# Second attention of a two-block layer: probabilities and values in rounded part and remainder, three rounded products for one fp32 product

## What is computed

```
def attend(args):
    qb, qc = args
    s = jnp.einsum('bqhd,bkhd->bhqk', qb, k).astype(jnp.float32) * scale
    mask = cid[None, :] <= qc[:, None]
    s = jnp.where(mask[None, None], s, neg)
    p = jax.nn.softmax(s, axis=-1).astype(v.dtype)
    return jnp.einsum('bhqk,bkhd->bqhd', p, v)
...
return o * jax.nn.silu(z)
...
y = jnp.concatenate([y_conv, y_mla, y_ret], axis=-1)
h = h + y @ w_out[l]
```

## Time and profile before

| | us |
|---|---|
| median of three runs (1928.8 to 1929.09) | 1928.89 |
| the profiled execution | 1929.18 |
| its span, first to last instruction | 1927.4 |
| PE busy in the span | 1859.5 |
| DVE busy | 1189.0 |
| ACT busy | 784.2 |
| POOL busy | 552.8 |

### The profile page before, as it was taken

One profiled execution on the slowest core, in us unless ns is written; L12 is line 12 of the kernel. 1 busy time (PEld: TensorE's weight loads), 2 busy tenths in 40 slices (PEclk: granted clock), 3 DMA queues, 4 the chain that ended last, 5 costly groups with the idle time before them and its releaser, 6 DMA issues.

```text
span 1927.4 us, 24207 instructions
## 1 busy us (share of the span) xinstructions
PE 1859.5 (96%) x9462; PEld 1512.4 (78%) x9462; DVE 1189.0 (62%) x1805; ACT 784.2 (41%) x1404; POOL 552.8 (29%) x554
## 2 busy tenths in 40 slices
PE   8999999899988999999999998999999998899999
PEld 5788788766777888887888887879988897676787
DVE  6678545555788666777877877455344348466642
ACT  6765223455543333333333354451211136455520
POOL 0120026440637565610000024560622134011100
PEclk9999999999999999999999999999999999899999
DMA  4143433300314535479555401113101314311131
GB/s 160 47 148 102 148 88 105 110 31 26 133 60 156 177 129 172 142 285 397 197 182 212 174 1 32 44 59 136 40 23 44 110 60 142 110 34 34 44 131 66
DMA packets 110026, 216.27 MB, mean 112 GB/s; under 512 B 37512, under 2 KB 42888, under 8 KB 105816
## 3 DMA queue, kind: packets, MB, share of 16 engines
q1 hardware_dynamic: 109624, 214.49, 32.8%
q10 hardware_dynamic: 288, 0.22, 0.0%
HBM read 153.82 MB, written 60.87 MB: 111 GB/s over the span
## 4 chain that ended last, share of the span: by engine, by line
PE 74%; DVE 10%; ACT 6%; POOL 4%; issue 3%; DMA 2%; SPq 0%; DVEq 0%; POOLq 0%; ACTq 0%
PE ps L361 10%; PE ps L362 9%; PE ps L363 9%; PE ps L1948 5%; PE ps L1950 5%; PE ps L1949 5%; PE ps L2336 5%; PE ps L2338 5%; PE ps L2337 5%; PE ps L3653 4%; PE ps L378 3%; PE ps L706 2%; ACT sc L1502 1%; PE ps L3554 1%; PE ps L3642 1%
## 5 line engine op out<-in xcount | busy, mean ns | idle before, releaser
L361 PE MATMUL ps<-xh,whi 128*128 128x512 f32 (+2 forms) x1160 | 458.3, 395 | 10.1 <-DVE wlo L330 6.4
L362 PE MATMUL ps<-xl,whi 128*128 128x512 f32 (+2 forms) x1160 | 442.9, 382 | 0.0
L363 PE MATMUL ps<-xh,wlo 128*128 128x512 f32 (+2 forms) x1160 | 442.1, 381 | 0.0
L361 PEld LDWEIGHTS ps<-xh,whi 128*128 128x128 f32 x1160 | 220.3, 190 | 59.6 <-issue 11.8
L363 PEld LDWEIGHTS ps<-xh,wlo 128*128 128x128 f32 x1160 | 219.9, 190 | 39.9
L362 PEld LDWEIGHTS ps<-xl,whi 128*128 128x128 f32 x1160 | 220.3, 190 | 33.1
L1948 PE MATMUL ps<-oph,wsh 128*128 128x512 f32 x448 | 177.2, 396 | 11.2 <-DVE stu L2066 6.0
L2336 PE MATMUL ps<-dnh_b,dnh_a 128*128 128x512 f32 x448 | 175.2, 391 | 5.0 <-DVE dn_b L2362 5.0
L1949 PE MATMUL ps<-opl,wsh 128*128 128x512 f32 x448 | 176.4, 394 | 0.0
L1950 PE MATMUL ps<-oph,wsl 128*128 128x512 f32 x448 | 176.2, 393 | 0.0
L2337 PE MATMUL ps<-dn_b,dnh_a 128*128 128x512 f32 x448 | 174.8, 390 | 0.0
(11 more groups left out here) (515 smaller groups left out, 3402.9 us busy)
## 6 DMA issues: line engine op xcount, KB each, us to landing
wraw<-panels SPq DMA_DIRECT2D x70, 512.0 KB, 3.6
dnr_b<-ff_d SPq DMA_DIRECT2D x28, 1024.0 KB, 7.5
dnr_a<-down SPq DMA_DIRECT2D x28, 1024.0 KB, 5.1
ff_d<-st SPq DMA_DIRECT2D x64, 256.0 KB, 5.9
ff_d<-stt SPq DMA_DIRECT2D x48, 256.0 KB, 5.9
upx<-up SPq DMA_DIRECT2D x16, 512.0 KB, 3.8
upy<-up SPq DMA_DIRECT2D x16, 512.0 KB, 5.5
hT<-x SPq DMA_DIRECT2D x8, 512.0 KB, 5.0
```

The lines of the kernel that those rows point to most:

```text
L361: pe.matmul(out, h, xh[:, xk, c0:c1_], start=(n == 0), stop=False)
L362: pe.matmul(out, h, xl[:, xk, c0:c1_], start=False, stop=False)
L363: mm = pe.matmul(out, l, xh[:, xk, c0:c1_], start=False, stop=(n == nk - 1))
```

## The change

Each unit is exponentiated twice by ACT: into a rounded buffer ("exp high", six buffers ph) and into an fp32 buffer (three pt). POOL subtracts one from the other and writes the remainder, rounded (three buffers pl, "p low"). The values of two heads are split once: ACT writes the rounded part vh, POOL the remainder vl, before head 0 and in slots 5 and 6 of heads 0, 2 and 4. PE makes high x high and high x low of unit j - 2 and the product of the low probabilities of unit j - 4 in each slot. The copies of sums move from ACT to DVE (slots 4 and 9), the inverses of half 1 to slots 5 to 8 and, in the last head, ahead of y_low of k = 0, 1 and 5; the ten early pieces of y move by four slots; POOL's multiplies are put between its subtractions; SP issues all eight hr loads after the last attention product. The lines of the changed kernel are 40 to 90 higher than before.

```diff
@@ -3501,7 +3501,14 @@
...
-    pts = [X(f"pt{i}", 37888 + 2048 * i, [512]) for i in range(4)]
+    pts = [X(f"pt{i}", 37888 + 2048 * i, [512]) for i in range(3)]
+    phs = [X("ph0", 44032, [512], F32R)] + [X(f"ph{i + 1}", 20096 + 2048 * i, [512], F32R) for i in range(5)]
+    pls = [X("pl0", 30336, [512], F32R)] + [X(f"pl{i + 1}", 59904 + 2048 * i, [512], F32R) for i in range(2)]
+    phs7 = [phs[0]] + [M(f"ph7{i}", 28 + 2 * i, [512], F32R) for i in range(5)]
+    pls7 = [M(f"pl7{i}", 38 + 2 * i, [512], F32R) for i in range(3)]
...
+    vhs = [X("vh0", 46080, [NB + 1, 3, 64], F32R), M("vh1", 80.1875, [NB + 1, 3, 64], F32R)]
+    vls = [X("vl0", 52992, [NB + 1, 3, 64], F32R), at("vl1", c_at, [NB + 1, 3, 64], F32R)]
...
+    def p_high(j):
+        return (phs7 if j // nu == 7 else phs)[j % 6]
+
+    def p_low(j):
+        return (pls7 if j // nu == 7 else pls)[j % 3]
...
+    def value_high_act(act, w, c):
...
+        step = 1 if c < 2 else 2
+        for n, bs in value_parts:
+            act.activation(vhs[c % 2][0:n, bs, 0:3:step, :], vm[0:n, bs, c, 0:3:step, :], ACT.Copy).then_inc(*act_at.up("vh", c, n))
+
+    def value_low_pool(pool, w, c):
...
+        step = 1 if c < 2 else 2
+        for n, bs in value_parts:
+            w.wait_ge(*act_at.at("vh", c, n))
+            pool.tensor_tensor(vls[c % 2][0:n, bs, 0:3:step, :], vm[0:n, bs, c, 0:3:step, :], vhs[c % 2][0:n, bs, 0:3:step, :].bitcast(F32), ALU.subtract).then_inc(*pool_at.up("vl", c, n))
...
-        def values(j):
+        def values_high(j):
             h, u = j // nu, j % nu
             hf, x, c0 = units[u]
+            c, n = h // 2, n_keys(x)
             if x == 0:
-                take(w, "values", ("o", h, hf), (act_at, ("o", h, hf)))
-            w.wait_ge(*act_at.at("exp", h, u))
-            w.wait_ge(*pool_la.at("ones"))
-            pe.matmul(tile("o", h, hf)[:, c0:512], values_of(h, x), pts[j % 4][0:n_keys(x), 0:512 - c0], start=(x == 0), stop=(x == last_x[hf])
-                      ).then_inc(*pe_at.up("values", j))
+                take(w, "values", ("o", h, hf), (dve_at, ("o", h, hf)))
+            w.wait_ge(*act_at.at("exp high", h, u))
+            w.wait_ge(*pool_at.at("vl", c, NMETA))
+            o = tile("o", h, hf)
+            pe.matmul(o[:, c0:512], vhs[c % 2][0:n, x, h % 2:h % 2 + 2, :], p_high(j)[0:n, 0:512 - c0], start=(x == 0), stop=False, skip_group_check=True)
+            pe.matmul(o[:, c0:512], vls[c % 2][0:n, x, h % 2:h % 2 + 2, :], p_high(j)[0:n, 0:512 - c0], start=False, stop=False, skip_group_check=True)
+
+        def values_low(j):
+            h, u = j // nu, j % nu
+            hf, x, c0 = units[u]
+            c, n = h // 2, n_keys(x)
+            w.wait_ge(*pool_at.at("p low", j))
+            pe.matmul(tile("o", h, hf)[:, c0:512], vhs[c % 2][0:n, x, h % 2:h % 2 + 2, :], p_low(j)[0:n, 0:512 - c0], start=False, stop=(x == last_x[hf]),
+                      skip_group_check=True).then_inc(*pe_at.up("values", j))
+                j = nu * h + u
                 scores(h, u)
-                if nu * h + u >= 2:
-                    values(nu * h + u - 2)
+                if j >= 2:
+                    values_high(j - 2)
+                if j >= 4:
+                    values_low(j - 4)
                 if h < 7:
                     for step in prepare[u]:
                         prepare_pe(pe, w, h + 1, *step)
-                elif u < 4:
-                    y_turn_pe(pe, w, *early[u])
-        values(8 * nu - 2)
-        values(8 * nu - 1)
+                elif 4 <= u < 8:
+                    y_turn_pe(pe, w, *early[u - 4])
+        values_high(8 * nu - 1)
+        for j in range(8 * nu - 3, 8 * nu):
+            values_low(j)
...
     def attend_act(act, w):
+        value_high_act(act, w, 0)
+        for h in range(8):
+            for u in range(nu):
+                hf, x, c0 = units[u]
+                j, n = nu * h + u, n_keys(x)
+                p = tile("unit", h, u)[0:n, 0:512 - c0]
+                w.wait_ge(*pe_at.at("unit", h, u))
+                if j > 5:
+                    w.wait_ge(*pe_at.at("values", j - 6))
+                act.activation(p_high(j)[0:n, 0:512 - c0], p, ACT.Exp).then_inc(*act_at.up("exp high", h, u))
+                if j > 2:
+                    w.wait_ge(*pool_at.at("p low", j - 3))
+                act.activation(pts[j % 3][0:n, 0:512 - c0], p, ACT.Exp).then_inc(*act_at.up("exp", h, u))
+                if h % 2 == 0 and h < 6 and u == 5:
+                    value_high_act(act, w, h // 2 + 1)
+                if h < 7:
+                    for step in prepare[u]:
+                        prepare_act(act, w, h + 1, *step)
+                elif 4 <= u < 4 + len(early):
+                    w.wait_ge(*pe_at.at("values", 7 * nu - 1))
+                    y_high_act(act, w, *early[u - 4])
+        for k in (0, 1, 5):
+            y_high_act(act, w, k, 0)
+
+    def attend_dve(dve, w):
                 w.wait_ge(*pool_at.at("y", h // 2 - 1, hf))
-            act.activation(den[hf][a:a + 64, :], p[b:b + 64, :], ACT.Copy).then_inc(*act_at.up("den", h, hf))
-            act.activation(og[hf][a:a + 64, :], p[a:a + 64, :], ACT.Copy).then_inc(*act_at.up("o", h, hf))
...
-                j = nu * h + u
...
-                act.activation(pts[j % 4][0:n_keys(x), 0:512 - c0], tile("unit", h, u)[0:n_keys(x), 0:512 - c0], ACT.Exp).then_inc(*act_at.up("exp", h, u))
-                if u == 2 and h > 0:
-                    summed(h - 1, 1)
-                if u == 7:
-                    summed(h, 0)
-                if h < 7:
-                    for step in prepare[u]:
-                        prepare_act(act, w, h + 1, *step)
-                elif u < len(early):
-                    y_high_act(act, w, *early[u])
-        for k in (0, 1, 5):
-            y_high_act(act, w, k, 0)
-        summed(7, 1)
-
-    def attend_dve(dve, w):
+            dve.tensor_copy(den[hf][a:a + 64, :], p[b:b + 64, :]).then_inc(*dve_at.up("den", h, hf))
+            dve.tensor_copy(og[hf][a:a + 64, :], p[a:a + 64, :]).then_inc(*dve_at.up("o", h, hf))
+
...
@@ -3708,29 +3767,61 @@
                 if h < 7:
                     for step in prepare[u]:
                         prepare_dve(dve, w, h + 1, *step)
-                if h > 0 and h % 2 == 0 and 3 <= u < 7:
-                    inverse(h // 2 - 1, 1, u - 3)
+                if u == 4 and h > 0:
+                    summed(h - 1, 1)
+                if u == 9:
+                    summed(h, 0)
+                if h > 0 and h % 2 == 0 and 5 <= u < 9:
+                    inverse(h // 2 - 1, 1, u - 5)
                 if h > 0 and h % 2 == 1 and u >= 10:
                     inverse(h // 2, 0, u - 10)
-                if h == 7 and u < len(early):
-                    y_low_dve(dve, w, *early[u])
+                if h == 7 and 4 <= u < 4 + len(early):
+                    y_low_dve(dve, w, *early[u - 4])
+        summed(7, 1)
+        for n in range(4):
+            inverse(3, 1, n)
         for k in (0, 1, 5):
             if k > 0:
                 w.wait_ge(*pe_at.end())
             y_low_dve(dve, w, k, 0)
-        for n in range(4):
-            inverse(3, 1, n)
 
     def attend_pool(pool, w):
-        for c in range(4):
...
+        def gated(c, hf):
...
+        value_low_pool(pool, w, 0)
+        for h in range(8):
+            for u in range(nu):
+                hf, x, c0 = units[u]
+                j, n = nu * h + u, n_keys(x)
+                w.wait_ge(*act_at.at("exp", h, u))
+                if j > 2:
+                    w.wait_ge(*pe_at.at("values", j - 3))
+                pool.tensor_tensor(p_low(j)[0:n, 0:512 - c0], pts[j % 3][0:n, 0:512 - c0], p_high(j)[0:n, 0:512 - c0].bitcast(F32), ALU.subtract
+                                   ).then_inc(*pool_at.up("p low", j))
+                if h % 2 == 0 and h < 6 and u == 6:
+                    value_low_pool(pool, w, h // 2 + 1)
+                if h % 2 == 1 and u == 11:
+                    gated(h // 2, 0)
+                if h > 0 and h % 2 == 0:
+                    if u == 1:
+                        divided(h // 2 - 1, 0)
+                    if u == 5:
+                        gated(h // 2 - 1, 1)
+                    if u == 9:
+                        divided(h // 2 - 1, 1)
+        divided(3, 0)
+        gated(3, 1)
+        divided(3, 1)
@@ -3838,11 +3929,9 @@
...
-        for n in range(3):
-            sp.dma_start(hr[n][:], h1_d[n]).then_inc(*ld_hr[n].up())
         sp_weights(sp, w, OUT0 + 3)
         w.wait_ge(*pe_at.end())
-        for n in range(3, 8):
+        for n in range(8):
             sp.dma_start(hr[n][:], h1_d[n]).then_inc(*ld_hr[n].up())
         for n in range(8):
```

More of the change, by code:

```diff
@@ L3720, in attend_dve, with divided @@
             y_low_dve(dve, w, k, 0)
[L3721 to L3722 removed]
     def attend_pool(pool, w):
[L3725 to L3733 removed]
+        def gated(c, hf):
+            z = zf2[:, c, 512 * hf:512 * hf + 512]
+            w.wait_ge(*dve_at.at("o", 2 * c + 1, hf))
```

(9 more changed lines are left out.)

40 lines of the change are left out of this document (23 added, 17 removed).

## The result

The changed kernel takes **1938.88 us** (median of 4 runs, 1937.92 to 1941.6) against 1928.85 for the kernel before beside it: ratio 1.0056, 95% interval 1.0044 to 1.0068. It is slower by 10 us; the prediction was 1930.1, with a range of 1921 to 1940. The time is inside the range, but by 1.1 us only: the range had been drawn to take in rivals that did not happen either. The case held likeliest (+1.2 us) is not what happened, and the 0.5% lies above the 0.2% that counted as no difference.

What follows compares the result with a forecast made beforehand. PE was taken to bound the kernel until another engine's queue is late. From 1929.2: heads -3.9, last head +0.5, output's start +3.1, half clock +1.5 give 1930.4 profiled, 1930.1 us as median; own range 1926 to 1933, with rivals 1921 to 1940.

Steps and rivals of the forecast that it cites:

- The case held likeliest: Whole kernel: the forecast's own sum of terms, 1930.1 us, no difference that can be told; chance 0.38.
- the two slower rivals: ACT sets the pace, exps 0.61 apart: 1935.0 us, chance 0.25; POOL does, subtractions from 1.5 us: 1940.5 us, chance 0.12.
- the idle of 2 to 3 us before the k = 0 block: Sign in the first output panel: PE idle, ended by xl, with granted clock 0.5 behind it; its absence means wrong.
- PE's own work: Attention heads: three rounded products replace one fp32 product, gaining 1.5 us a head, 12 us over eight heads.
- the faster rival: Heads bound by PE alone: other engines' waits vanish and each of eight heads gains 1.5 us; 1921.5 us, chance 0.25.
- Slots 0 to 4 come to 7.7: Start of each head: 6.95 of PE work, 0.65 wait for kl, 0.1 small waits, against 8.4: -0.7 us a head.
- PE waits 0.8 in even, 0.35 in odd heads: Slots 5 to 13: DVE's copies delay the maxima PE wants for its turn, and in odd heads also the shift.
- values_low(10) waits 1.35: Heads 2 and 4: POOL's subtractions bunch with gated, value_low and divided, so PE waits 1.35 us for the low product.
- The last head: +0.5: Head 7: 16.8 us of PE work, but POOL, with gated ahead of sub(12) and sub(13), ends at 19.5; products at 20.0.
- The output's start: +3.1 and +1.5: First output panel: y_low late behind DVE's sums and reciprocals, +3.1 us; half clock after PE's idle, +1.5 us.
- hr loads: nothing: Output stage: issuing all eight hr loads after the last attention product costs nothing; a load 7 us longer would remove the cover.
- the POOL rival: POOL sets the pace: multiplies beside DVE work take 1.71 us and subtractions likewise; 1940.5 us, chance 0.12.

Runs made afterwards that it cites:

- e11: Changed kernel, half-0 sums at slot 11, last head with one fp32 product and ScalarE's sums, value_low in odd heads, split in head 1, early y two per slot: 1924.63 us.
- e1: Changed kernel with VectorE's copies of half-0 sums moved from slot 9 to behind the shift in slot 11 of heads 0 to 6: 1933.82 us.
- e9: e1 with POOL's value_low of the next pair moved from slot 6 of heads 0, 2, 4 to slot 6 of heads 1, 3, 5: 1930.7 us.
- e3: Changed kernel with POOL's gated(3, 0) moved from slot 11 of the last head to behind all subtractions: 1943.05 us.
- e4: Changed kernel with e1's and e3's edits, plus y_low(0) and y_low(1) ahead of VectorE's last copies and reciprocals: 1932.84 us.

## Why the prediction was right and wrong

The forecast sum was +1.2 us over the kernel before, the trace shows +9.9. That 1938.9 still lies in the range is luck: it stands between the times of the two slower rivals (1935.0 and 1940.5), whose mechanisms, an exp step of 0.61 and subtractions of 1.5 us or more, did not occur. Of the prediction's own signs, the steps of products, exps and subtractions came as forecast; slots 5 to 13 took 13.9 to 14.3 us in place of 12.6 to 13.5, and the idle of 2 to 3 us before the k = 0 block, whose absence was to show it wrong, was absent. By its terms:

- **PE's own work: right in mechanism, too large.** Splitting is worth 0.17 us for 512 columns, and with the waits gone (e11) heads 2 and 3 take 21.08 and 20.95 against 21.81 and 22.03: 0.7 and 1.1 us, where 1.5 was reckoned. (The prediction's own sums for a head, 20.65 and 19.55, are 1.1 apart and not 1.5; its forecast went by 19.55, the faster rival by 1.5.) The slots of head 3, from start to start of scores:

```
slot          0    1    2    3    4    5    6    7    8    9    10   11   12   13
before       1.62 1.55 1.74 1.85 1.71 1.43 1.26 1.90 1.90 1.98 1.74 1.43 0.82 1.08
changed      2.00 1.73 1.43 1.86 1.71 1.53 1.42 1.61 1.64 1.82 1.57 2.22 1.05 1.02
e11          1.50 1.73 1.43 1.85 1.71 1.54 1.41 1.62 1.64 1.82 1.57 1.35 1.06 0.72
```

- **"Slots 0 to 4 come to 7.7": failed.** They take 8.2 even in e11, 8.3 in even heads and 8.7 in heads 3 and 5 of the changed kernel. The wait for kl is 0.28 there, as before, and not 0.65: ScalarE's doubled exps did not make kh late. But without it PE still takes 7.95 from start to start, where 6.95 and 0.1 of small waits were reckoned. I had counted 0.9 us of small gaps as waits that faster products would close, while the products themselves, of units 12, 13, 0, 1 and 2, could gain 0.4 there by the prediction's own prices, and gained 0.1 in even and 0.25 in odd heads. Slots 3 and 4 stay at 1.85 and 1.71 in every row above, the slots with kT's transposes and the wait for kl; what sets them was not taken apart. This step was most of the forecast gain of heads 0 to 6. The extra 0.5 of slot 0 in heads 3 and 5 is POOL.
- **"PE waits 0.8 in even, 0.35 in odd heads": right place, too small.** The waits are 1.16 to 1.41 and 0.77 to 0.79, 6.1 us in all. A 64x512 copy takes 0.69 (step 0.72), so it goes by columns and not by partitions, 10 to 20% over my 0.6 to 0.65. For odd heads I had reckoned 0.2 at the turn; but DVE is busy without a pause for 3.6 us from the next to last pair on, as in even heads, where a reciprocal more is in the run. e1 shows that these waits are worth 5 us.
- **"values_low(10) waits 1.35" in heads 2 and 4: right, hidden.** In the changed kernel the wait at the turn lets POOL catch up, and 0.26 is left of it at the start of head 3 (1731.53). With the turn's wait gone it is there, 0.94 (e1), and goes when value_low moves (e9): 3.1 us.
- **"The last head: +0.5": failed, +3.5.** I let POOL end at 19.5 us and had named gated ahead of sub(12) and sub(13), but reckoned with pieces at their own pace. Beside VectorE's y pieces the subtractions of 512, 512, 448 and 320 columns take 5.59, where their means are 4.65 together (1.29, 1.29, 1.17, 0.90), gated takes 1.84 and not 1.28, and the last two 1.30, means 0.93: 1.9 us of the 2.9 that POOL is late. The last products come 22.1 us after the head's start; e3 shows gated's place to be worth 2.0. The other 1.0 us lies ahead of 1834.29: three subtractions in a row start after idles of 0.41, 0.34 and 0.20 us for ScalarE's exps, and ScalarE has no pause of more than 0.1 us from 1826.7 on. This is the "multiplies beside DVE work" of the POOL rival, in one place and not in the pace of a head.
- **The output's start: +3.1 and +1.5 forecast, +3.2 measured, of another make.** 2.7 us is half clock on the five blocks ahead of k = 0, and 0.5 lies behind it, at k = 1 (the wait for y_low(1)). I took the idle that starts the half clock to be the one for y_low(0); the one for POOL's last differences came first. y_low(0) itself was ready at about 1849.1 (1848.42 + 0.68, as in e3, where the k = 0 block starts 0.68 behind the pair), 5.9 us after the last value product; I had said 6.1.
- **hr loads: nothing**, as forecast; PE's distance from the second panel to the end is 79.55 in both.

The rule of exclusive access that the prediction quoted from the Trainium skill (SBUF — State Buffer, "SBUF: two separate sides") can now be set beside rows that tell it apart. In e3 a multiply starts 0.09 us ahead of a y piece and takes its 1.27; the y piece takes 1.73, about 0.62 and what was left of the multiply. With the order turned, the y pieces start at 1849.28 (e3) and the multiply 0.16 later: PE's k = 0 block starts at 1849.96, so the first y piece was undisturbed, the multiply takes 1.59, and the pair 2.30. The 2.39 of the earlier trace rows is of this kind, with this row of POOL beside it, 0.06 us behind:

```profile
1836.43 1.78 POOL L3733 TENSOR_TENSOR zf<-zf,den 128x512 f32<-128x512 f32 x1 [5.53 <-DVE den L3704]
```

That one of the two goes undisturbed and the other waits for its end agrees with these rows. That it is the one that starts first can't be read from starts 0.1 us apart: in the changed kernel gated starts 0.10 us ahead of a y piece too (1839.85 and 1839.95), and there the y piece takes its 0.62 and gated 1.84.

The chances: of the prediction's rivals the one that ends faster (PE alone) is close to e11, where the waits were taken away by hand, though it keeps 0.7 to 1.1 of the 1.5 us a head. No rival had "VectorE sets the pace of every head and POOL the last one", the case that happened.

## What to carry to other kernels

When work moves from an idle engine to one with slack on average, look at the stretch between what that engine is given last and what the bound engine wants first: here 1.4 us of copies in a busy run of 3.6 us cost 5 us in all, and two slots later they made no wait at the turn. A new helper engine keeps up only if its other pieces are spread: with a 2.4 us piece in full heads the same subtraction load cost 3 us more than with it in the emptier ones, where heads 2 to 5 had no wait for it, and at the end of a stage, where no later work of the bound engine covers a lag, the old single product was the better one. Take waits away together: one removed alone uncovered the next one in e1 and e3, and three together still did in e4.
